# Expert pairs: wide weights by indirect gather, gathers without padding rows, gate and up products from f32r parts

## The chip, the cores and the metric

The kernel runs on one core of one Trainium2 chip. The metric is the device time of one execution in microseconds (us). Before the change three runs gave a median of 3015.25 us (3013.92 to 3015.65).

## The reference

Two transformer-like blocks work on 1024 tokens of width 1024, in float32. Each block is a mixer (a state-space scan and a Fourier mixer in the first, an S5 branch and a gated unit in the second) followed by a mixture of experts with 32 experts in 4 groups. The change is in the two mixtures only. Each token goes to the two best experts of its best group, so there are 2048 assignments per block, and every expert computes, for the rows it is given:

```python
p_top_grp, grp = lax.top_k(p_grp, 1)            # best of 4 groups
p_top, j_top = lax.top_k(p_exp, TOP_K_INNER)    # best 2 of its 8 experts
gate = p_top_grp * p_top / jnp.sum(p_top, axis=-1, keepdims=True)
hid = silu(xblk @ w_gate[e]) * (xblk @ w_up[e])     # 1024 -> 512
y = hid @ w_down[e]                                 # 512 -> 1024
out[token] += gate * y
```

Each expert has three weights of 2 MB (w_eg, w_eu, w_ed in the first block, w1, w3, w2 in the second).

## The kernel before

Everything runs in program order per engine with semaphores written out by hand; there is no planner. `moe_phase` (first block) and `mixed_moe` (second block) compute the routing: TensorE makes logits, VectorE a long chain of small steps that ends in the lists `idx_a` and `idx_b` (which rows to gather) and `ids` (which expert each unit of work takes), stored to `blk_dram`. Both then call `expert_pairs` (L1078 to L1346).

The assignments are cut into units. A wide unit has 128 rows, a narrow unit 64. A pair is one wide unit of one expert and one narrow unit of another, 192 row slots; slots with no assignment are padding and hold row 0. There are 18 pairs in the first block and 17 in the second; the count is read at run time (`pairs`).

The weights of a pair are nine pieces in nine buffers: `w_a[0..2]` (gate, up, down of the wide unit, 2 MB each) and `w_b[0..5]` (gate, up, down of the narrow unit, in halves of 1 MB). The pieces of the first pair are loaded during the routing. In the loop SP issues all nine, in one queue and a fixed order: wide gate, wide up, four narrow pieces, wide down, two narrow pieces. Each issue waits until the buffer has been used (`s_used`, or `s_wdl` for wide down).

TensorE does per pair: gate and up of the wide unit (`up_a`, float32 products of 128x512, each two passes, L1192), gate and up of the narrow unit (`up_b`, L1202), transposes of the hidden values and of the next wide rows (`rows_a`), the wide down product (`down_a`), the narrow down product (`down_b`), transposes of the next narrow rows (`rows_b`).

`down_a` already works from f32r parts: ScalarE copies the weight piece to f32r (`wd_h`, L1291), VectorE subtracts that from the piece (`wd_l`, L1326), and TensorE adds three f32r products: high by high, high by low, low by high (L1215, L1216, L1221).

VectorE also makes `hid_a` (L1323), which happens once per pair when gate and up are done, copies the transposed rows to SBUF (`rows_T`), and scales the results (`y_a` L1342, `y_b` L1345), which ScalarE stores to `yrows`. POOL gathers the rows of the next pair from `xr_dram` with two indirect DMAs (L1152).

Of the kernel before, what the change touches and what calls it, by code (L numbers as in the profile page):

```python
# [6 lines left out]
P = 128  # L7
D = 1024
SEQ = 1024
T = SEQ // P  # L10
# [9 lines left out]
POOL_DMA_SEMAPHORES = 6  # L20
# [18 lines left out]
def moe_phase(nc, tag, x_in, mod, norm_w, w_rg, b_rg, w_re, b_re, w_gate, w_up, w_down, yrows, pool_dma, keep):  # L39
# [11 lines left out]
    s_xb, s_ga = pool_dma[0:2], pool_dma[2:6]  # L51
    xr_half = xr_dram.rearrange("s (h d) -> (s h) d", h=2)
    with ExitStack() as ctx:
# [15 lines left out]
        idx_a, idx_b = (sb(n, [P, NB], I32) for n in ("idxa", "idxb"))  # L69
        x_a, x_b = sb("xa", [P, D]), sb("xb", [P, D // 2])  # L70
        w_a = [sb(f"wa{p}", [P, 2 * WF]) for p in range(3)]
        w_b = [sb(f"wb{p}", [P, WF]) for p in range(6)]
        s_wa = [sem(f"wa{p}") for p in range(3)]
        s_wb = [sem(f"wb{p}") for p in range(6)]
        ga_dram, ua_dram = (w.rearrange("e (p j) f -> e p (j f)", j=J) for w in (w_gate, w_up))
        gb_dram, ub_dram = (w.rearrange("e (h p j) f -> e h p (j f)", h=2, j=J // 2) for w in (w_gate, w_up))
        da_dram = w_down.rearrange("e (p c) d -> e p (c d)", c=JF)
        db_dram = w_down.rearrange("e (h p c) d -> e h p (c d)", h=2, c=2)

        def piece_a(e, p):  # L80
            return (ga_dram, ua_dram, da_dram)[p][e]
# [4 lines left out]
        with ExitStack() as c2:  # L86
# [59 lines left out]
            isbig, upper = sb2("isbig", [P, 1]), sb2("upper", [P, 1])  # L146
            idf = sb2("idf", [P, 4])
# [5 lines left out]
            ps_f = ps_q[:, 1, 0:2 * NB].rearrange("p (c i) -> p c i", c=2)  # L153

# [21 lines left out]
            s_ft, s_fi, s_step = sem("ft"), sem("fi"), sem("step")  # L176
# [3 lines left out]
            with nc.Block() as block:  # L180
                @block.sync
                def _(sp):
# [24 lines left out]
                def _(pool):  # L207
# [4 lines left out]
                    nc.gpsimd.iota(tokf[:, :], [[P, T]], base=0, channel_multiplier=1,  # L212
# [11 lines left out]
                    nc.gpsimd.tensor_copy(wr[:, :, NG:NG + NE].rearrange("p j (g e) -> p g j e", g=NG), wre[:, :, :, :]).then_inc(s_wrc, 1)  # L224
                    for r in range(RXS):
                        pool.wait_ge(s_sr[r], 16 * (T // RXS))
                    pool.wait_ge(s_fi, 2)
                    nc.gpsimd.indirect_dma_start(x_a[:, :], None, xr_dram,
                                                 bass.IndirectOffsetOnAxis(ap=idx_a[:, 0:1], axis=0)).then_inc(s_xb[0], 16)
                    nc.gpsimd.indirect_dma_start(x_b[:, :], None, xr_half,  # L230
                                                 bass.IndirectOffsetOnAxis(ap=idx_b[:, 0:1], axis=0)).then_inc(s_xb[1], 16)
# [35 lines left out]
                def _(pe):  # L267
# [48 lines left out]
                    last.then_inc(s_ft, 1)  # L316

                @block.vector
                def _(v):
# [141 lines left out]
                    link(nc.vector.tensor_scalar(upper[:, :], iota_p[:, :], SB - 0.5, None, ALU.is_gt))  # L461
# [14 lines left out]
                    nc.vector.tensor_copy(ids[:, :], idf[:, :]).then_inc(s_blk, 1)  # L476

        expert_pairs(nc, tag, w_a, w_b, s_wa, s_wb, piece_a, piece_b, NE, NF, xr_dram, xr_half, blk_dram, yrows, ident, s_xb, sem, idx_a, idx_b, x_a, x_b, mod[5 * D:6 * D])
# [3 lines left out]
def mixed_moe(nc, tag, mix, mod, norm_w, w_rg, b_rg, w_re, b_re, w_gate, w_up, w_down, final_w, x_out, yrows, pool_dma):  # L482
# [11 lines left out]
    s_xb, s_ga = pool_dma[0:2], pool_dma[2:6]  # L494
    xr_half = xr_dram.rearrange("s (h d) -> (s h) d", h=2)
    with ExitStack() as ctx:
# [12 lines left out]
        idx_a, idx_b = (sb(n, [P, NB], I32) for n in ("idxa", "idxb"))  # L509
        WF = J // 2 * NF  # L510
# [20 lines left out]
        with ExitStack() as c2:  # L531
# [52 lines left out]
            with nc.Block() as block:  # L584
                @block.sync
                def _(sp):
# [30 lines left out]
                def _(pool):  # L617
# [17 lines left out]
                    for r in range(RXS):  # L635
                        pool.wait_ge(s_sr[r], 16 * (T // RXS))
# [3185 lines left out]
```

## Time and profile before

| | |
|---|---|
| median of the runs | 3015.25 us |
| the profiled execution | 3012.52 us, span 3010.8 us |
| mean granted TensorE clock | 0.949 |
| TensorE busy | 2716.9 us, 90% of the span |
| VectorE busy | 1446.9 us, 48% |
| ScalarE busy | 768.4 us, 26% |
| POOL busy | 204.9 us, 7% |
| bytes moved by DMA | 799.95 MB, mean 266 GB/s |
| share of SP's queue | 694.08 MB, 60.8% of 16 engines |
| software queue (POOL) | 45.88 MB, 4.1% |

Busy times are sums of instructions; DMA shares are of the 16 DMA engines over the whole span. The expert loops stand out in the page's slices as two stretches (about 1020 to 1620 us and 2400 to 2960 us) with TensorE and DMA both near full.

### The profile page before, as it was taken

Reading aid. Unit: us, or ns where it says so; the run is one execution under the profiler, and the core shown is the slowest. Engines: PE = TensorE matmul, PEld = TensorE weight load, DVE = VectorE, ACT = ScalarE, POOL = GpSimd, SP = SyncE. Lnnn points to the kernel's source line nnn. Section 1 sums busy time; section 2 is a strip of 40 time slices with the busy share of each in tenths; the row PEclk is TensorE's granted clock in tenths of the full one; section 3 lists DMA queues with packets and bytes.
Section 4 is the critical chain, followed back from the end, with each engine's and each line's share of the span. In section 5 each row is a group of like instructions: output and inputs, shape, how many; then the busy total and the mean of one; then the engine's idle time right before and its main releaser. Section 6 shows DMA issues by size and latency. Waiting matters only on the chain. (4 is left out here: it accounts for less than half of the span.)

```text
span 3010.8 us, 36671 instructions
## 1 busy us (share of the span) xinstructions
PE 2716.9 (90%) x13982; PEld 1892.5 (63%) x13982; DVE 1446.9 (48%) x2054; ACT 768.4 (26%) x1116; POOL 204.9 (7%) x242
## 2 busy tenths in 40 slices
PE   4999996988798799999997899799779799999998
PEld 2788784765577555555553587688657655555554
DVE  3766365896633533332333755573445533323334
ACT  4223222653302012111212521234212121112112
POOL 0000000000000000000001121121000000000002
PEclk6999997999899899999998899899899899999999
DMA  6652374787734699999996414353652599999996
GB/s 244 243 179 77 104 270 144 221 266 283 271 116 178 273 424 425 424 424 426 425 424 251 127 50 108 77 125 108 234 193 99 220 395 424 424 425 426 424 424 252
DMA packets 276482, 799.95 MB, mean 266 GB/s; under 512 B 34164, under 2 KB 156592, under 8 KB 229784
## 3 DMA queue, kind: packets, MB, share of 16 engines
q1 hardware_dynamic: 234368, 694.08, 60.8%
q10 hardware_dynamic: 29112, 58.54, 5.3%
q0 software_dynamic: 12896, 45.88, 4.1%
q8 instruction: 71, 1.16, 0.2%
q14 instruction: 35, 0.29, 0.0%
HBM read 684.76 MB, written 113.67 MB: 265 GB/s over the span
## 5 line engine op out<-in xcount | busy, mean ns | idle before, releaser
L1192 PE MATMUL m_ps_ga<-m_wa,m_xTa 128*128 128x512 f32 x560 | 250.1, 600 | 0.8 <-issue 0.8
L1202 PE MATMUL m_ps_b<-m_wb,m_xTb 128*64 128x256 f32 x2240 | 249.5, 381 | 0.0
L1323 DVE TENSOR_TENSOR m_hida<-m_ps_ua,m_sila 128x512 f32<-128x512 f32 x35 | 24.2, 691 | 463.9 <-PE m_ps_ua L1192 463.9
L1192 PE MATMUL m_ps_ua<-m_wa,m_xTa 128*128 128x512 f32 x560 | 246.0, 592 | 0.0
L1763 PE MATMUL xp_acc<-xp_xh,xp_wh 128*128 128x512 f32 (+3 forms) x600 | 223.7, 373 | 6.9 <-DVE xp_xl L2046 6.9
L1288 ACT ACT_TABLE_LOAD x35 | 44.9, 1283 | 702.8 <-PE m_ps_ga L1192 702.8
L1202 PEld LDWEIGHTS m_ps_b<-m_wb,m_xTb 128*64 128x64 f32 x2240 | 157.8, 137 | 102.3 <-issue 26.5
L1764 PE MATMUL xp_acc<-xp_xl,xp_wh 128*128 128x512 f32 (+3 forms) x600 | 221.3, 369 | 0.0
L1765 PE MATMUL xp_acc<-xp_xh,xp_wl 128*128 128x512 f32 (+3 forms) x600 | 221.2, 369 | 0.0
L2942 PE MATMUL xq_acc<-xq_xh,xq_wh 128*128 128x512 f32 x448 | 181.2, 404 | 13.6 <-PEq L3011 6.4
L1192 PEld LDWEIGHTS m_ps_ua<-m_wa,m_xTa 128*128 128x128 f32 x560 | 106.4, 190 | 133.9 <-issue 133.9
L1326 DVE TENSOR_TENSOR m_wdl<-m_wa,m_wdh 128x2048 fp32r<-128x2048 f32 x70 | 157.1, 2286 | 62.6 <-ACT m_wdh L1291 62.6
L1192 PEld LDWEIGHTS m_ps_ga<-m_wa,m_xTa 128*128 128x128 f32 x560 | 105.5, 194 | 121.0 <-issue 121.0
L2943 PE MATMUL xq_acc<-xq_xl,xq_wh 128*128 128x512 f32 x448 | 178.8, 399 | 0.0
L2944 PE MATMUL xq_acc<-xq_xh,xq_wl 128*128 128x512 f32 x448 | 178.6, 399 | 0.0
L1291 ACT ACTIVATE m_wdh<-m_wa 128x2048 fp32r<-128x2048 f32 x70 | 130.0, 1904 | 169.8 <-DMA m_wa<-in_w_ed_dram 94.3
L1763 PEld LDWEIGHTS xp_acc<-xp_xh,xp_wh 128*128 128x128 f32 (+1 forms) x600 | 112.6, 188 | 29.4 <-issue 9.6
L1231 PE MATMUL m_ps_b<-m_wb,m_hTb 128*64 128x512 f32 x560 | 127.9, 598 | 0.0
L1215 PE MATMUL m_ps_y<-m_wdh,m_hTah 128*128 128x512 f32 x280 | 116.0, 414 | 10.7 <-DVE m_hTah L1329 10.6
L1765 PEld LDWEIGHTS xp_acc<-xp_xh,xp_wl 128*128 128x128 f32 (+1 forms) x600 | 112.5, 187 | 20.3
L1764 PEld LDWEIGHTS xp_acc<-xp_xl,xp_wh 128*128 128x128 f32 (+1 forms) x600 | 112.7, 188 | 19.8
L1216 PE MATMUL m_ps_y<-m_wdl,m_hTah 128*128 128x512 f32 x280 | 109.8, 392 | 0.0
(706 smaller groups left out, 4770.0 us busy)
## 6 DMA issues: line engine op xcount, KB each, us to landing
m_wa<-in_w_dram SPq DMA_DIRECT2D x51, 2048.0 KB, 17.5
m_wb<-in_w_dram SPq DMA_DIRECT2D x102, 1024.0 KB, 17.9
m_wa<-in_w_eg_dram SPq DMA_DIRECT2D x18, 2048.0 KB
m_wa<-in_w_eu_dram SPq DMA_DIRECT2D x18, 2048.0 KB, 16.3
m_wb<-in_w_eg_dram SPq DMA_DIRECT2D x36, 1024.0 KB, 17.4
m_wb<-in_w_eu_dram SPq DMA_DIRECT2D x36, 1024.0 KB, 22.2
m_wa<-in_w_ed_dram SPq DMA_DIRECT2D x18, 2048.0 KB, 26.8
m_wb<-in_w_ed_dram SPq DMA_DIRECT2D x36, 1024.0 KB, 20.7
```

The lines of the kernel that those rows point to most:

```text
L1192: last = nc.tensor.matmul(out[:, :], xT_a[:, j, :], w[:, k, :], start=(j == 0), stop=(j == J - 1))
L1202: last = nc.tensor.matmul(ps_b[c * SB:(c + 1) * SB, p // 2, :], xT_b[:, k, h * SB:(h + 1) * SB], w[:, k, c * HF:(c + 1) * HF], start=(h == ...
L1215: nc.tensor.matmul(o, hT_ah[:, k, :], w_h[:, c, cols], start=(k == 0), stop=False)
L1231: last = nc.tensor.matmul(ps_b[d * SB:(d + 1) * SB, :, :], hT_b[:, c, h * SB:(h + 1) * SB], w[:, c, d * NF:(d + 1) * NF], start=(k == 0), ...
L1291: nc.scalar.activation(wd_h[:, h, :], w_a[2][:, h * WF:(h + 1) * WF], ACT.Copy).then_inc(s_wdh, 1)
L1326: nc.vector.tensor_tensor(wd_l[:, h, :], w_a[2][:, h * WF:(h + 1) * WF], wd_h[:, h, :].bitcast(F32), ALU.subtract).then_inc(s_wdl, 1)
L1763: nc.tensor.matmul(o, h, xh[:, j, a:a + w], start=(j == 0), stop=False)
L1764: nc.tensor.matmul(o, h, xl[:, j, a:a + w], start=False, stop=False)
L1765: last = nc.tensor.matmul(o, l, xh[:, j, a:a + w], start=False, stop=(j == J - 1))
L2942: nc.tensor.matmul(o, wh[:, n % 2, j, :], x_h[:, j, tok], start=(j == 0), stop=False)
L2943: nc.tensor.matmul(o, wh[:, n % 2, j, :], x_l[:, j, tok], start=False, stop=False)
L2944: last = nc.tensor.matmul(o, wl[:, n % 2, j, :], x_h[:, j, tok], start=False, stop=(j == k - 1))
```

## The change

In `expert_pairs` and the two functions that call it:

- The wide pieces are no longer issued by SP. POOL gathers each with an indirect DMA: 128 rows of 16 KB, at row numbers `idx_w` (expert times 128 plus partition). Where a pair's wide expert is that of the pair before, or the pair is past the last, the number is made larger than the table, and an indirect DMA with `bounds_check` leaves such rows out. `idx_w` is made by a few more steps at the end of the routing (`spread`, `weight`, `again`). The first pair's wide pieces are gathered by POOL too.
- Padding slots of `idx_a` and `idx_b` now hold a number past the table (`PAD`), so that the gathers leave them out; `x_a` and `x_b` are set to zero once beforehand.
- Gate and up of the wide unit are computed from f32r parts, as down was. The two-slot buffer `wd_h`, `wd_l` becomes a ring (`ring_h`, `ring_l`) through which six halves go per pair: gate, up, down, two each. ScalarE makes the high part, VectorE the low part; a slot is filled again when TensorE has used it (`s_ring`). The first two halves of the next pair's gate are made at the end of a pair. The rows `xT_a` become `xT_ah` and `xT_al`.

The core of the diff:

```diff
@@ routing, both blocks
-                    nc.vector.tensor_copy(idx_a[:, :], ps_f[:, 0, :]).then_inc(s_fi, 1)
+                    nc.vector.tensor_scalar(idx_a[:, :], ps_f[:, 0, :], float(PAD), None, ALU.add).then_inc(s_fi, 1)
...
+                    nc.vector.tensor_scalar(spread[:, :], ident[:, 0:NB], idf[:, 0:1], None, ALU.mult).then_inc(s_spread, 1)
+                    v.wait_ge(s_we, 1)
+                    link(nc.vector.tensor_scalar(weight[:, :], ps_e, float(P), iota_p[:, 0:1], ALU.mult, ALU.add))
+                    link(nc.vector.tensor_tensor(again[:, 1:NB], weight[:, 1:NB], weight[:, 0:NB - 1], ALU.is_equal))
+                    link(nc.vector.scalar_tensor_tensor(out=again[:, 1:NB], in0=iota_s[:, 1:NB], scalar=npair[:, 0:1],
+                                                        in1=again[:, 1:NB], op0=ALU.is_ge, op1=ALU.add))
+                    link(nc.vector.scalar_tensor_tensor(out=idx_w[:, 1:NB], in0=again[:, 1:NB], scalar=8.0 * NE * P,
+                                                        in1=weight[:, 1:NB], op0=ALU.mult, op1=ALU.add))
...
@@ POOL during the routing
+                    for p in range(3):
+                        nc.gpsimd.indirect_dma_start(w_a[p][:, :], None, wide[p],
+                                                     bass.IndirectOffsetOnAxis(ap=first[:, 0:1], axis=0)).then_inc(s_wa[p], 16)
+                    nc.gpsimd.memset(x_a[:, :], 0.0).then_inc(s_zero, 1)
+                    nc.gpsimd.memset(x_b[:, :], 0.0).then_inc(s_zero, 1)
...
@@ expert_pairs, SP
-                    e_a = sp.value_load(blk_dram[0:1, bass.ds(4 * i, 1)], min_val=0, max_val=NE - 1)
-                    for p in range(2):
-                        sp.wait_ge(s_used, 12 * i + 2 * p + 2)
-                        sp.dma_start(w_a[p][:, :], piece_a(e_a, p)).then_inc(s_wa[p], 16)
...
-                    sp.wait_ge(s_wdl, 2 * i)
-                    sp.dma_start(w_a[2][:, :], piece_a(e_a, 2)).then_inc(s_wa[2], 16)
...
@@ expert_pairs, POOL
+                def weights(i, p):
+
+                    pool.wait_ge(s_wl, 6 * i + 2 * p + 8)
+                    pool.sem_inc(s_one, 1)
+                    nc.gpsimd.tensor_copy(row_w[p][:, :], idx_w[:, bass.ds(i + 1, 1)]).then_inc(s_rw[p], 1)
+                    pool.wait_ge(s_rw[p], i + 1)
+                    pool.sem_inc(s_one, 1)
+                    pool.indirect_dma_start(w_a[p][:, :], None, wide[p], bass.IndirectOffsetOnAxis(ap=row_w[p][:, :], axis=0),
+                                            bounds_check=NE * P - 1, oob_is_err=False).then_inc(s_wa[p], 16)
+
+                gather(1, 1, idx_a, row_a, xr_dram, x_a, s_xta, 0, SEQ)
+                with pool.Fori(0, n) as i:
+                    gather(i + 1, i + 1, idx_b, row_b, xr_half, x_b, s_xtb, 1, 2 * SEQ)
+                    for p in range(3):
+                        weights(i, p)
+                    gather(i + 2, i + 2, idx_a, row_a, xr_dram, x_a, s_xta, 0, SEQ)
...
@@ expert_pairs, TensorE
+                    for h in range(2):
+                        w_h, w_l = (w[:, h, :].rearrange("p (j f) -> p j f", f=NF) for w in (ring_h, ring_l))
+                        pe.wait_ge(s_wh, 6 * i + 2 * u + h + 1)
+                        for k in range(J // 2):
+                            j = h * J // 2 + k
+                            nc.tensor.matmul(out[:, :], xT_ah[:, j, :], w_h[:, k, :], start=(j == 0), stop=False)
+                            nc.tensor.matmul(out[:, :], xT_al[:, j, :], w_h[:, k, :], start=False, stop=False)
+                        pe.wait_ge(s_wl, 6 * i + 2 * u + h + 7)
+                        for k in range(J // 2):
+                            j = h * J // 2 + k
+                            last = nc.tensor.matmul(out[:, :], xT_ah[:, j, :], w_l[:, k, :], start=False, stop=(j == J - 1))
+                        last.then_inc(s_ring, 1)
...
@@ expert_pairs, ScalarE (in the loop)
+                    act.wait_ge(s_wa[1], 16 * i + 16)
+                    for h in range(2):
+                        act.wait_ge(s_ring, 6 * i + h + 1)
+                        high(1, h)
                     act.wait_ge(s_hida, i + 1)
                     nc.scalar.activation(sil_a[:, :], ps_ga[:, :], ACT.Silu).then_inc(s_sila, 1)
                     act.wait_ge(s_wa[2], 16 * i + 16)
                     for h in range(2):
+                        act.wait_ge(s_ring, 6 * i + h + 3)
+                        high(2, h)
...
                     nc.scalar.activation(sil_b[:, :], ps_b[:, 0, :], ACT.Silu).then_inc(s_silb, 1)
+                    act.wait_ge(s_wa[0], 16 * i + 32)
+                    act.wait_ge(s_ring, 6 * i + 5)
+                    high(0, 0)
+                    act.wait_ge(s_ring, 6 * i + 6)
+                    high(0, 1)
                     act.wait_ge(s_ya, i + 2)
...
@@ expert_pairs, VectorE (low: ring_l = w_a piece - ring_h)
+                    for h in range(2):
+                        low(1, h, 6 * i + h + 2)
+                    low(2, 0, 6 * i + 4)
...
                     nc.vector.tensor_tensor(hid_a[:, :], ps_ua[:, :], sil_a[:, :], ALU.mult).then_inc(s_hida, 1)
+                    low(2, 1, 6 * i + 5)
...
-                    rows_T(ps_x[:, :, :], xT_a, i + 1, s_xta, s_xTa)
+                    wide_T(i + 1)
...
                     nc.vector.tensor_tensor(y_a[:, :], ps_y[:, :], g2a[:, :], ALU.mult).then_inc(s_ya, 1)
+                    low(0, 0, 6 * i + 6)
...
+                    low(0, 1, 6 * i + 7)
```

## Rows read from the trace of the kernel before

**Rows 1.** DMA issues by line: tiles, queue, operation, count, KB, median us to landing.
```profile
m_wa<-in_w_dram SPq DMA_DIRECT2D x51, 2048.0 KB, 17.5
...
m_wa<-in_w_ed_dram SPq DMA_DIRECT2D x18, 2048.0 KB, 26.8
...
m_xa<-m_xr,m_rowa POOLq DMA_INDIRECT x35, 9.1
```

**Rows 2.** Windows in the first loop: stretch, busy us per engine, clock, DMA share, GB/s.
```profile
1200.00:1300.00 100.00, 100.00 (x485) 55.97 (x486) 33.59 (x34) 17.93 (x16) 6.95 (x12) 1.00 1.01 425
...
1500.00:1600.00 100.00, 97.86 (x466) 54.45 (x464) 32.62 (x33) 18.00 (x16) 6.95 (x12) 1.00 1.01 425
```

**Rows 3.** Timeline of VectorE, both loops: start, duration, instruction, idle before it.
```profile
1037.18 0.69 DVE L1323 TENSOR_TENSOR m_hida<-m_ps_ua,m_sila 128x512 f32<-128x512 f32 x1 [15.78 <-PE m_ps_ua L1192]
...
1069.76 0.69 DVE L1323 TENSOR_TENSOR m_hida<-m_ps_ua,m_sila 128x512 f32<-128x512 f32 x1 [13.11 <-PE m_ps_ua L1192]
...
1330.69 0.69 DVE L1323 TENSOR_TENSOR m_hida<-m_ps_ua,m_sila 128x512 f32<-128x512 f32 x1 [13.11 <-PE m_ps_ua L1192]
...
1346.03 1.22 DVE L1342 TENSOR_TENSOR m_yra<-m_ps_y,m_g2a 128x1024 f32<-128x1024 f32 x1 [2.42 <-PE m_ps_y L1221]
...
1364.01 0.69 DVE L1323 TENSOR_TENSOR m_hida<-m_ps_ua,m_sila 128x512 f32<-128x512 f32 x1 [13.11 <-PE m_ps_ua L1192]
...
2941.65 0.69 DVE L1323 TENSOR_TENSOR m_hida<-m_ps_ua,m_sila 128x512 f32<-128x512 f32 x1 [13.11 <-PE m_ps_ua L1192]
```

**Rows 4.** Waits, 1060 to 1600 us: who for whom, us in total, times, longest.
```profile
ACT m_wdh L1291 <- DMA m_wa<-in_w_ed_dram: 94.3, 17, 7.1
```

**Rows 5.** End of the first loop: timeline, and one window.
```profile
1597.13 7.13 PE L1202 MATMUL m_ps_b<-m_wb,m_xTb 128*64 128x256 f32 x64
1597.33 0.69 DVE L1323 TENSOR_TENSOR m_hida<-m_ps_ua,m_sila 128x512 f32<-128x512 f32 x1 [13.11 <-PE m_ps_ua L1192]
...
1616.01 0.75 PE L1183 MATMUL m_ps_x<-m_ident,m_xb 128*128 128x128 f32 x4
...
1605.00:1610.00 5.00, 4.34 (x24) 3.61 (x23) 3.73 (x6) 0.00 (x0) 0.00 (x0) 1.00 0.00 0
```

**Rows 6.** Timeline of TensorE, gate and up of one pair.
```profile
1088.32 7.03 PE L1192 MATMUL m_ps_ga<-m_wa,m_xTa 128*128 128x512 f32 x16
...
1102.15 2.16 PE L1202 MATMUL m_ps_b<-m_wb,m_xTb 128*64 128x256 f32 x18
```

**Rows 7.** Timeline of TensorE, first and last of ten product starts in `down_a`.
```profile
1306.91 0.40 PE L1216 MATMUL m_ps_y<-m_wdl,m_hTah 128*128 128x512 f32 x1
...
1308.96 0.63 PE L1221 MATMUL m_ps_y<-m_wdh,m_hTal 128*128 128x512 f32 x2
```

**Rows 8.** Groups by line, 1130 to 1650 us: busy us, mean ns, idle before.
```profile
L1326 DVE TENSOR_TENSOR m_wdl<-m_wa,m_wdh 128x2048 fp32r<-128x2048 f32 x30 | 67.4, 2287 | 36.0 <-ACT m_wdh L1291 36.0
L1291 ACT ACTIVATE m_wdh<-m_wa 128x2048 fp32r<-128x2048 f32 x30 | 55.7, 1905 | 91.1 <-DMA m_wa<-in_w_ed_dram 91.1
L1288 ACT ACT_TABLE_LOAD x14 | 18.0, 1283 | 262.8 <-PE m_ps_ga L1192 262.8
L1152 POOL DMA_INDIRECT m_xb<-m_xr,m_rowb x14 | 13.8, 983 | 11.0 <-POOL m_rowb L1149 11.0
L1152 POOL DMA_INDIRECT m_xa<-m_xr,m_rowa x14 | 13.6, 969 | 11.2 <-POOL m_rowa L1149 11.2
```

**Rows 9.** Timeline ahead of the loops, first block, then second.
```profile
1009.14 1.15 POOL L228 DMA_INDIRECT m_xa<-m_xr,m_idxa  x1 [56.15 <-DVE m_idxb L465]
...
1010.32 0.33 ACTq L263 DMA_DIRECT2D m_blk<-m_ids  x1
...
1016.23 1.95 PE L1237 MATMUL m_ps_x<-m_ident,m_xa 128*128 128x128 f32 x8 [8.45 <-PEq L180]
...
1021.10 3.78 PE L1192 MATMUL m_ps_ga<-m_wa,m_xTa 128*128 128x512 f32 x4 [0.42 <-issue]
...
2400.36 8.94 PE L1192 MATMUL m_ps_ga<-m_wa,m_xTa 128*128 128x512 f32 x16 [0.38 <-issue]
```

More of the change, by code:

```diff
@@ L146, in moe_phase @@
             isbig, upper = sb2("isbig", [P, 1]), sb2("upper", [P, 1])
+            spread, weight, again = (sb2(n, [P, NB]) for n in ("spread", "weight", "again"))
             idf = sb2("idf", [P, 4])
@@ L316, in _ @@
                     last.then_inc(s_ft, 1)
+                    pe.wait_ge(s_spread, 1)
+                    nc.tensor.matmul(ps_e, ones[:, :], spread[:, :], start=True, stop=True).then_inc(s_we, 1)
                 @block.vector
@@ L509, in mixed_moe @@
         idx_a, idx_b = (sb(n, [P, NB], I32) for n in ("idxa", "idxb"))
+        idx_w, first = sb("idxw", [P, NB], I32), sb("first", [P, 1], I32)
         WF = J // 2 * NF
@@ L547, in mixed_moe @@
                 sb2(n, [P, NE]) for n in ("nbig", "nsml", "thr", "bend", "send", "bst", "sst", "sbase", "bbase", "early"))
-            half, npair, over, gain, later, isbig, upper = (sb2(n, [P, 1]) for n in ("half", "npair", "over", "gain", "later", "isbig", "upper"))
+            half, npair, over, gain, later, isbig, upper = (
+                sb2(n, [P, 1]) for n in ("half", "npair", "over", "gain", "later", "isbig", "upper"))
+            spread, weight, again = (sb2(n, [P, NB]) for n in ("spread", "weight", "again"))
             idf, ids = sb2("idf", [P, 4]), sb2("ids", [P, 4], I32)
@@ L731, in _ @@
                     last.then_inc(s_ft, 1)
+                    pe.wait_ge(s_spread, 1)
+                    nc.tensor.matmul(ps_e, ones[:, :], spread[:, :], start=True, stop=True).then_inc(s_we, 1)
                 @block.vector
@@ L1106, in expert_pairs @@
         s_used = sem("used")
-        s_row = [sem(f"row{r}") for r in range(2)]
+        s_row, s_rw = [sem(f"row{r}") for r in range(2)], [sem(f"roww{p}") for p in range(3)]
+        s_sta, s_stb = sem("sta"), sem("stb")
         s_xta, s_xtb, s_xTa, s_xTb = (sem(k) for k in ("xta", "xtb", "xTa", "xTb"))
@@ L1162, in _ @@
-                for r in range(2):
-                    pool.wait_ge(s_xb[r], 16 * n + 16)
+                    pool.indirect_dma_start(x[:, :], None, src, bass.IndirectOffsetOnAxis(ap=row[:, :], axis=0),
+                                            bounds_check=rows - 1, oob_is_err=False).then_inc(s_xb[r], 16)
+                def weights(i, p):
[6 more added lines that the diff above has]
+                                            bounds_check=NE * P - 1, oob_is_err=False).then_inc(s_wa[p], 16)
```

189 lines of the change are left out of this document (106 added, 83 removed).

## The prediction

> **What bounds the kernel now.** I read, in this order, the windows, the timeline of VectorE, the timeline of TensorE inside a pair, the landing times of the DMAs, and the end of a loop. The change touches the two expert loops (18 pairs in the first block, 17 in the second, counted by the issues: 18 of the first block's down weights, 51 for the second's three wide pieces [rows 1]). In the windows the reader is to see two engines full at once: TensorE 98 to 100 of 100 us at a granted clock of 1.00, and DMA share 1.01 at 425 GB/s [rows 2]. Which one ends last is told by the distance between two `m_hida` instructions, one per pair: 32.6 us at first (1069.76 less 1037.18), 33.3 us from the tenth pair on (1364.01 less 1330.69) [rows 3]. 33.3 us is the DMA pace: a pair moves nine weight pieces, 12.58 MB, gathers 192 rows (0.79 MB) and stores as many, 14.16 MB, and at 425 GB/s that is 33.3 us. 32.6 us is TensorE's own pace, while the weights loaded ahead last. Where TensorE then waits is seen in ScalarE's wait for the down piece (94.3 us in 17 pairs) and in that piece's landing of 26.8 us [rows 1, 4]: its parts must be split before `down_a`. At the end of the loop DMA is already empty from 1605 on, while products run to 1616.8 [rows 5]: the one queue finishes early because its late piece is not the last one.
>
> **The change part by part, one pair.**
>
> *Gate and up from parts.* Now the two take from 1088.32 to 1102.15, 13.83 us (32 passes, 0.43 us each) [rows 6]. Afterwards they are 48 f32r products; the same kind in `down_a` follows each 0.228 us (1306.91 to 1308.96, nine steps) [rows 7]: 10.94 us. That takes 2.9 us from TensorE's 32.6. The price is four more ACT copies of 1.91 us and four more DVE subtractions of 2.29 us per pair, and one more subtraction for `xT` (1.22 us, as `m_yra` of the same size) [rows 3, 8]. ACT goes from about 6 to 14 us per pair and DVE from 11 to 21, sums from these rows, so neither is full; but the ring holds two halves, so a half can be split only when the one before the last is used up. That chain is copy 1.91, subtraction 2.29 and some 0.4 of semaphores, 4.6 us; a half lasts 12 x 0.228 = 2.74 us, and the low parts are wanted after another 8 x 0.228 = 1.82, that is after 4.56. The two meet to 0.1 us. I charge 0.2 us per pair, bounds 0 and 1.4 (a table load of 1.28, now ahead of silu [rows 8], falling into the chain). TensorE's pace: 32.6 - 2.9 + 0.2 = 29.9, taken as 30.0.
>
> *Bytes.* Counting the reference's routing on the inputs that it draws gives 2048 real rows in each block, against 18 x 192 and 17 x 192 gathered, and two pairs of the first block (the 10th and the 12th) whose wide expert is that of the pair before, none in the second. A pair then moves 12.58 + 0.79 stored + 0.47 to 0.49 gathered = 13.84 MB: 32.6 us, still more than 30.0. So DMA stays the bound, 0.7 us quicker per pair, except around a repeated expert, which leaves out 6.29 MB (14.8 us).
>
> *Where the pieces come free.* A wide piece is now free when its second low half is made, not when the products have read it: the gate buffer right at the start of a pair instead of 7 us later, the up buffer at 10, down at 17. Each has its own wait in POOL's queue, so the wide pieces no longer stand in line with the narrow ones in SP's. A wide gather is not in the trace. On POOL the nearest are the row gathers, 0.97 us with rows of 4 KB, 0.98 with 2 KB [rows 8], so the time goes by rows, not bytes: I take 1.0 us plus copy and wait of 1.1, bounds 1.0 and 3.9 (a row split in four); five gathers keep POOL under half of the pair. In its queue `gather` of the next wide rows stands behind the wait for the down piece, at 17 us, but those rows are wanted a pair later. On ScalarE the copies of the next gate piece stand ahead of the y stores, and behind their wait for that piece wait only these stores, which VectorE asks for a pair later; SP only loses issues. Landing: between 4.9 us (2 MB at full rate) and 26.8 (the down piece in SP's line). I take 10.5, from the x_a gather: 128 packets of 4 KB on the software queue land in 9.1 us although SP's queue is full [rows 1]; that is 8 packets per engine, each taking turns with one of 8 or 16 KB (0.3 to 0.6 us at a sixteenth of 425 GB/s), plus some 3 us fixed. Eight packets of 16 KB: 8 x (0.6 + 0.3) + 3. The Trainium skill, "DMA: Bandwidth & Descriptors", section on queues, rings and completion order, says that each DMA engine goes round the queues that have work, a packet each. The trace agrees, 9.1 against 26.8 us at the same load; strict order by issue would give the last rival's time.
>
> *Slack.* The gate piece must land about 20 us after it is freed (its copies follow `down_a`), up and down 20 to 22; 12.6 with the issue fits. So the narrow pieces, in SP's queue with what DMA is left, are late first: the fourth one, last of `up_b`. DMA works without a gap from about 14 us after the first gate product (until then it has moved one wide piece and two gathers, 2.9 MB). By then the second pair's fourth narrow piece needs about 9 MB, 21 us, so it lands at 35 to 36; it is wanted at 2.1 (cold first pair: 1021.10 to 1037.18 less 0.2, against 13.83 [rows 3, 6, 9]) + 30.0 + 10.9 + 5.4 = 48.4. Slack 12 us, shrinking by 2.6 per pair.
>
> *Before the loops.* The extra `xT` subtraction stands ahead of the first gate product: 2400.36 moves by 1.2 us, twice [rows 9]. The five small DVE steps and one product for `idx_w` (1.8 us by their like) run while the block list is stored and the engines meet, 1010.3 to 1016.2 [rows 9]: nothing, 3.6 us in both blocks if uncovered. POOL's iota, memsets and three first gathers lie in the 56 us that POOL waits for the indices [rows 9]: nothing, and below nothing is excluded, since the indices end that wait. The 12.58 MB loaded ahead are the same.
>
> **Sum, from the profiled execution's 3012.5 us (span 3010.8).** First block: now 1021.10 to 1616.76, 595.7 us. After: 1.2 + 2.1 + 18 x 30.0 = 543.3, plus waits for DMA: slack 12 is gone by the seventh pair, 6 us by the ninth; filled to 12 again at the tenth and twelfth, 3.5 us by the eighteenth. 552.8: 42.9 less. Second block: now 2400.36 to 2961.1 (the last `m_hida` at 2941.65 plus the 19.4 it has to the end in the first block, 1597.33 to 1616.76 [rows 3, 5]), 560.7. After: DMA throughout. 16 x 12.58 MB of weights, 12.6 of stores, 8.0 of gathers are 222 MB; less 2.9 moved early and 2.1 (two last pieces) 217 MB, 510.9 us; plus 14, plus 14.3 from the fourth narrow piece to the end (19.6 less three quarters of 7.13 [rows 5]), plus 1.2: 540.4, 20.3 less. Together 63: 2949.3, and 2952 on the scale of the runs, whose median is 2.7 above the profiled execution.
>
> **Rivals.**
>
> *The split sets the pace*: the table load or a late copy costs 1.4 us per pair, 31.4. First block 3.3 + 18 x 31.4 = 568.5, no DMA wait; second 3.3 + 17 x 31.4 + 6.5 of DMA waits = 543.6. Less 44: 2971. For it: 0.1 us of room. Against: today's copies need no load of their own [rows 8]. The Trainium skill, "GPSIMD Engine Reference", key points, says that POOL shares its SBUF interfaces with VectorE and contends with instructions of two SBUF inputs. The new subtractions are such; by that rule two of them per pair, each held up for most of a gather's 0.97 us, would give this rival's time. No row shows a gather beside one.
>
> *Skipped rows still cost their transfer* (the change does not do what it says): pace 33.3 again; first block 543.3 + 41, second 513.3 + 38. Less 21, from the earlier buffers alone: 2994. No row shows an index out of range.
>
> *Slower: a wide buffer's round is longer than the pair.* Each wide piece has one buffer: freed, issued 2.1, landed L, copied in two halves, subtracted: L + 8.7. With L = 26.8 as the down piece today [rows 1] 35.5 us for each pair that is not a repeat: 36 + 15 x 35.5 + 2 x 30 and 34 + 16 x 35.5 against 1156.4, 74 slower: 3089. It decides from L = 24.4 on. Against it the 9.1 us of the row gathers; for it that 2 MB have never gone through this queue.
>
> **Numbers.** Forecast 0.53, split 0.16, no skip 0.11, slower 0.12, the rest (mixtures, a few per cent less DMA rate) 0.08. The forecast's own range is 2932 (slack 20 instead of 12) to 2968. The range 2930 to 3000 takes in the first two rivals. Within 0.2% (6 us, what a measurement can tell) 0.03; faster 0.84; slower 0.13.
>
> **What would show it.** `m_hida` distances of 30 us, then 32.6, 30 again after the 10th pair; in the second block 32.6 from the seventh on; DMA at 425 GB/s; gate and up in 11 us; wide gathers landing in 10 to 14 us; software-queue bytes up by some 195 MB. Distances of 33 throughout, landings over 24 us, or waits of gate products for `ringl` would prove it wrong.

## The result, and the profile after

The changed kernel takes 2985.4 us (median of four runs, 2983.0 to 2986.9); the kernel before took 3014.6 in the same session. The ratio is 0.990, 95% interval 0.9888 to 0.9912: 29 us faster, where 63 were forecast. The profiled execution took 2986.4 us (span 2984.6).

Two parts came out as predicted. The first is the bytes. The page's queues of the kernel after (queue: packets, MB, share of 16 engines):

```profile
q1 hardware_dynamic: 219248, 473.87, 43.8%
q0 software_dynamic: 29168, 241.21, 19.7%
```

The software queue carries 195 MB more, as forecast. The second is that the wide pieces land soon enough. The landings (tiles, queue, operation, count, KB where given, median us), which answer to [rows 1]:

```profile
m_wb<-in_w_dram SPq DMA_DIRECT2D x102, 1024.0 KB, 24.5
m_wb<-in_w_ed_dram SPq DMA_DIRECT2D x36, 1024.0 KB, 23.3
m_wa<-in_w_dram,m_roww POOLq DMA_INDIRECT x51, 14.3
m_xa<-m_xr,m_rowa POOLq DMA_INDIRECT x37, 16.3
```

A wide gather lands in 14.3 us (10.5 taken, 24.4 would have made the kernel slower), a narrow piece of half the size only in 24. By the rule of the Trainium skill that the prediction drew on ("DMA: Bandwidth & Descriptors", queues and rings: a packet from each queue in turn) a queue of 16 KB packets would get twice what a queue of 8 KB packets gets, if what the rule calls a packet is what the profile counts as one. 2 MB in 14.3 against 1 MB in 24.5 us goes that way, but it is no test: a narrow piece also stands behind those issued before it in SP's queue.

The loops look otherwise than forecast. Windows of the kernel after, as [rows 2] (stretch, busy us of PE, PEld, DVE, ACT, POOL, granted clock, DMA share, GB/s):

```profile
1100.00:1200.00 100.00, 96.76 (x538) 66.25 (x534) 63.78 (x49) 45.20 (x31) 28.41 (x31) 0.97 1.01 425
1300.00:1400.00 100.00, 100.00 (x562) 70.00 (x558) 67.68 (x54) 47.12 (x32) 31.92 (x33) 1.00 0.90 351
1500.00:1600.00 100.00, 92.50 (x516) 64.48 (x514) 66.88 (x52) 46.09 (x34) 29.21 (x32) 0.98 0.82 336
2500.00:2600.00 100.00, 93.80 (x504) 63.31 (x503) 63.19 (x48) 43.58 (x30) 25.33 (x30) 0.95 1.01 421
```

DMA share 1.01 and TensorE with gaps: a loop that waits for DMA. Only about the two repeats of block 1 (1300 to 1400) is it the other way round. (The third row reaches past the end of the loop at 1592.5, so its lower DMA share is not the loop's.) VectorE's `m_hida`, one per pair, as [rows 3], and then the issue of the last two narrow pieces, and TensorE between the second and third of these `m_hida`:

```profile
1096.62 0.68 DVE L1412 TENSOR_TENSOR m_hida<-m_ps_ua,m_sila 128x512 f32<-128x512 f32 x1
1127.02 0.68 DVE L1412 TENSOR_TENSOR m_hida<-m_ps_ua,m_sila 128x512 f32<-128x512 f32 x1
...
1163.46 0.68 DVE L1412 TENSOR_TENSOR m_hida<-m_ps_ua,m_sila 128x512 f32<-128x512 f32 x1
```
```profile
1111.13 2.05 SPq L1175 DMA_DIRECT2D m_wb<-in_w_ed_dram  x2
```
```profile
1139.53 1.94 PE L1287 MATMUL m_ps_b<-m_wb,m_hTb 128*64 128x512 f32 x8
1144.71 3.68 PE L1287 MATMUL m_ps_b<-m_wb,m_hTb 128*64 128x512 f32 x8 [3.24 <-DMA m_wb<-in_w_ed_dram]
1148.32 1.13 PE L1234 MATMUL m_ps_x<-m_ident,m_xb 128*128 128x128 f32 x4
```

A pair takes 30.4 us (1127.02 less 1096.62) or, where it waits, 36.4 (1163.46 less 1127.02). What is late is the last narrow down half, issued at 1111 to 1113 and landed at 1144.7. After the 3.24 us wait the same eight products take 3.68 us in place of 1.94: the granted clock is 1.00 before the wait (1139.5 to 1141.5) and 0.50, the lower of its two levels (1.2 and 2.4 GHz), from 1144.7 to 1149.5. Distances of block 1 from the first pair on: 30.1, 30.4, 30.4, **36.4**, 30.2, **35.6**, 30.2, **37.3**, six of 30.1 to 30.4, **36.5**, 30.1, 30.4. In block 2 they go between 30.1 and 37.1 throughout, mean 32.64. The rows of the waits (who for whom, us, times, longest, 1060 to 1600 us), where [rows 4] had ScalarE's 94.3 us (the first is POOL waiting for the subtraction that frees a wide buffer):

```profile
POOL m_roww L1197 <- DVE m_ringl L1396: 113.8, 34, 4.6
...
PEld m_ps_b L1287 <- DMA m_wb<-in_w_ed_dram: 17.6, 5, 4.3
...
PE m_ps_b L1287 <- DMA m_wb<-in_w_ed_dram: 13.4, 4, 3.4
```

The end of the second loop, as [rows 5]: VectorE's last `m_hida` and TensorE's last products of the loop, then the window of DMA (in its second row a share of 0.23 and 89 GB/s: the tail of what had been 424):

```profile
2918.76 0.68 DVE L1412 TENSOR_TENSOR m_hida<-m_ps_ua,m_sila 128x512 f32<-128x512 f32 x1
```
```profile
2934.95 0.75 PE L1234 MATMUL m_ps_x<-m_ident,m_xb 128*128 128x128 f32 x4
```
```profile
2905.00:2915.00 10.00, 9.91 (x43) 7.71 (x43) 7.64 (x5) 7.29 (x6) 6.43 (x4) 1.00 1.03 424
2915.00:2935.00 20.00, 20.00 (x127) 12.87 (x125) 13.12 (x12) 7.65 (x5) 3.61 (x6) 1.00 0.23 89
```

From first gate product to last product, block 1 went from 595.7 to 571.8 us (1020.75 to 1592.5), block 2 from 560.7 to 555.6 (2380.13 to 2935.7); what lies between the blocks grew by 4.0. Forecast were 552.8 and 540.4, each with 1.2 for what stands ahead of the loop.

### The profile page after: what moved, and what is told of

The parts are those of the page before. It is cut to its first block and busy times, and to the rows that moved or that the text cites. A ratio compares the mean times of both kernels' runs of the same rounds, so it can differ in the third digit from the quotient of the medians.

```text
span 2984.6 us, 39013 instructions
## 1 busy us (share of the span) xinstructions
PE 2659.2 (89%) x14546; PEld 2003.0 (67%) x14546; DVE 1818.7 (61%) x2245; ACT 1089.5 (37%) x1295; POOL 461.6 (15%) x468
## 5 line engine op out<-in xcount | busy, mean ns | idle before, releaser
L1396 DVE TENSOR_TENSOR m_ringl<-m_wa,m_ringh 128x2048 fp32r<-128x2048 f32 x214 | 489.3, 2287 | 142.8 <-ACT m_ringh L1340 141.8
L1340 ACT ACTIVATE m_ringh<-m_wa 128x2048 fp32r<-128x2048 f32 x214 | 409.6, 1915 | 287.2 <-PE m_ps_y L1277 184.1
L1287 PE MATMUL m_ps_b<-m_wb,m_hTb 128*64 128x512 f32 x560 | 142.2, 646 | 31.1 <-DMA m_wb<-in_w_dram 17.7
L3020 POOL TENSOR_TENSOR xq_wl<-xq_raw,xq_wh 128x1024 fp32r<-128x1024 f32 (+1 forms) x32 | 78.2, 2444 | 361.0 <-ACT xq_wh L3015 361.0
L1244 PE MATMUL m_ps_ga<-m_ringh,m_xTah 128*128 128x512 f32 x280 | 118.3, 422 | 2.4 <-issue 2.4
L1187 POOL COPY m_rowb<-m_idxb 128x1 int32 x35 | 69.4, 1983 | 322.5 <-PE m_ps_x L1234 322.5
L1271 PE MATMUL m_ps_y<-m_ringh,m_hTah 128*128 128x512 f32 x280 | 116.4, 416 | 0.0
L2024 DVE TENSOR_TENSOR xp_wl<-xp_raw,xp_wh 128x1024 fp32r<-128x1024 f32 (+1 forms) x29 | 34.7, 1197 | 132.0 <-ACT xp_wh L1933 132.0
L1245 PE MATMUL m_ps_ga<-m_ringh,m_xTal 128*128 128x512 f32 x280 | 113.9, 407 | 0.0
L1287 PEld LDWEIGHTS m_ps_b<-m_wb,m_hTb 128*64 128x64 f32 x560 | 37.6, 143 | 110.8 <-issue 68.4
## 6 DMA issues: line engine op xcount, KB each, us to landing
m_wb<-in_w_dram SPq DMA_DIRECT2D x102, 1024.0 KB, 24.5
m_wb<-in_w_ed_dram SPq DMA_DIRECT2D x36, 1024.0 KB, 23.3
```

The costliest lines, as they stand in the source:

```text
L1244: nc.tensor.matmul(out[:, :], xT_ah[:, j, :], w_h[:, k, :], start=(j == 0), stop=False)
L1271: nc.tensor.matmul(o, hT_ah[:, k, :], w_h[:, c, cols], start=(k == 0), stop=False)
L1287: last = nc.tensor.matmul(ps_b[d * SB:(d + 1) * SB, :, :], hT_b[:, c, h * SB:(h + 1) * SB], w[:, c, d * NF:(d + 1) * NF], start=(k == 0), ...
L1340: nc.scalar.activation(ring_h[:, h, :], w_a[p][:, h * WF:(h + 1) * WF], ACT.Copy).then_inc(s_wh, 1)
L1396: nc.vector.tensor_tensor(ring_l[:, h, :], w_a[p][:, h * WF:(h + 1) * WF], ring_h[:, h, :].bitcast(F32), ALU.subtract).then_inc(s_wl, 1)
```

## The experiments

Three theories stood at first. **1, order**: the wide pieces come early, the narrow down halves late, so the reserve lies in the wrong pieces. **2, bytes**: the DMA engines are full, and only the byte count matters. **3, split and clock**: the chain of copies and subtractions and TensorE's lower clock make the long pairs. "Loop 1" and "loop 2" below are the time from a block's first `m_hida` to its last, from the profiled execution; the kernel before had 560.2 and 525.4, the one after 539.6 and 522.2. Ratios are to the kernel before on the same chip. The edits are shown in short form: each line stands for its counterpart in the kernel, and helper lines are left out.

**One queue in order of need** (wide pieces from SP again; then the same with a branch past a repeated expert's loads):

```diff
+ for p in range(2): sp.wait_ge(s_wl, 6 * i + 2 * p + 2); sp.dma_start(w_a[p], piece_a(e_a, p))
  for p in range(4): sp.wait_ge(s_used, 6 * i + p + 1);  sp.dma_start(w_b[p], piece_b(e_b, p))
+ sp.wait_ge(s_wl, 6 * i + 6); sp.dma_start(w_a[2], piece_a(e_a, 2))
  for p in (4, 5): ...
```

> The changed kernel with the wide pieces issued by SP again, in one queue with the narrow ones and in the order in which they are needed (gate, up, four narrow, down, two narrow); a repeated expert is loaded again. Theory 1 (two queues put the reserve in the wrong pieces: the wide ones come early, the narrow down halves late): the first pairs of block 1 go at 30.4 us, no 36 us pair before the eighth, and TensorE hardly waits for the narrow down halves (17.6 us after, under 5 here); block 2 ends some 9 us earlier, because the last piece to land is needed later; block 1 pays up to 15 us for the two repeats (6.29 MB at 420 GB/s). Sum 2980 to 2992. Theory 2 (bytes at the rate of the DMA engines are the bound, the order does nothing): 2985.4 + 15 = 3000. Theory 3 (the chain of the split and the lower clock set the pace, not the DMAs): 2985, with pairs of 36 us left where they are.

> The one queue in order of need, and SP branches past the three wide loads of a repeated expert (it adds 16 to the semaphore in their place). Theory 1 (order of the pieces): block 1 loses the stalls ahead of the repeats, about 13 us, block 2 about 9 us of its tail and up to 4 us more if the one queue moves 425 GB/s in place of 421: 2958 to 2965. Theory 2 (bytes and rate alone, which are those of the changed kernel): 2985, within 4 us. Theory 3 (split chain and clock): 2985, within 4 us.

Measured: 2995.3 (ratio 0.9945, 0.9933 to 0.9957), loops 555.0 and 524.1; with the branch 2990.0 (0.9922, 0.9909 to 0.9935), loops 545.3 and 526.4. Theory 1 fails: the narrow down halves are no longer late, and nothing is won; with the same bytes the kernel with the branch is some 6 us slower than the changed one. The wait moved to the wide pieces (first row, the kernel with one queue, 2450 to 2850 us), and the long pairs became even ones of 33.3 us, at a clock of 1.00 and the same full DMA (second row, window of the one with the branch). These two kernels change more than the order, though: in SP's one queue a piece whose buffer is free stands behind one whose buffer is not, and in the first pairs of the one with the branch DMA moves only 365 and 370 GB/s (1035 to 1060 and 1060 to 1080 us), against 402 and 428 in the changed kernel.

```profile
ACT m_ringh L1351 <- DMA m_wa<-in_w_dram: 60.3, 11, 5.9
```
```profile
2500.00:2600.00 100.00, 91.41 (x511) 63.12 (x510) 62.86 (x49) 44.44 (x30) 13.44 (x13) 1.00 1.01 424
```

That also takes the clock out: 0.95 in the same stretch of the changed kernel, 1.00 here, and loop 2 no shorter. The lower clock follows the waits (0.50 after the 3.24 us wait above); where it stays at 1.00, no time is won.

**Nothing wide to load** (every index out of bounds), and **the two queues held in order** (POOL waits for the fifth narrow piece's landing ahead of the gate gather):

```diff
- again = (weight[1:] == weight[:-1])
+ again = (weight[1:] == weight[1:])
```
```diff
+ if p == 0: pool.wait_ge(s_wb[4], 16 * i + 16)
```

> The changed kernel with every wide index of the loops out of bounds, so that no wide weights are loaded after the first pair (all pairs are computed with the first expert's wide weights). It shows TensorE's own pace with the split, beside DMA engines that have half as much to move. Theories 1 and 2 (DMA sets what is above 30.4 us a pair): all pairs at 30.2 to 30.6 us, granted clock 1.0 in both loops, 2985 - 24 (excess over 30.4 in block 1) - 36 (block 2) = 2925. Theory 3 (split chain and clock): pairs of 34 to 37 us remain, over 2960.

> The changed kernel with one more wait on POOL: the gate gather of the next pair is issued only when the fifth narrow piece of this pair has landed, so the two queues keep nearly the order of need and the skip stays. Theory 1: the narrow down halves land earlier (median landing under 20 us in place of 22, none over 30), the 36 us pairs ahead of the repeats go, block 2 gains less than with one queue: 2965 to 2975. Theories 2 and 3: 2985, within 4 us, or slower, since the wide pieces start later.

Without wide loads: all distances 30.1 to 30.7 us in both loops, means 30.37 and 30.46, clock 1.00. Time 2961.9, but its changed rows give block 2 an 18th pair; less 30.5 that is 2931, against 2925 expected. Theory 3 falls: the split alone keeps 30.4. Row of its window:

```profile
1350.00:1450.00 100.00, 100.00 (x552) 68.47 (x552) 69.45 (x54) 48.68 (x32) 30.61 (x31) 1.00 0.67 250
```

The held queues: 3018.6 (1.0015, 1.0004 to 1.0027), loops 558.1 and 535.1: some 35 us slower than the changed kernel, 44 to 54 beyond what theory 1 gave. DMA moves 401 to 415 GB/s in the stretches of block 2, where the changed kernel has 417 to 426; that fits a queue that is left with less to do by each wait for a landing.

**The parts alone.** Split without the byte savings (one queue, no skip, `PAD = 0`), and byte savings without the split (gate and up as before, wide pieces and rows by the changed gathers):

> Gate and up from f32r parts, and nothing else of the change: wide pieces by SP in one queue, no repeated expert left out, padding rows gathered again, so the bytes are those of the kernel before. Theory A (the DMA engines, busy without a gap, set the time; order and queue change nothing): TensorE's pace falls from 32.6 to 30.4 us a pair and nothing comes of it, every pair takes 33.3 us (14.15 MB at 425 GB/s): 3008 to 3016. Theory B (the parts are worth something each, and add up): it shows a good part of the 29 us, 3000 or less.

> The gathers, the skip and the left-out padding rows of the change, with gate and up in plain fp32 as before. Theory A: TensorE's pace of 32.6 us a pair is now the bound, so only what before had over 32.6 goes (the pairs of 33.3: 6 us in block 1, 4 in block 2): 3002 to 3008, all pairs within 0.1 of 32.6, DMA share under 1. Theory B: with the f32r part alone it adds up to the 29 us of both.

Measured: split alone 3017.5 (1.0004, 0.9996 to 1.0013): nothing. Bytes alone 3008.7 (0.9974, 0.9965 to 0.9984): 8 us. Together they give 30 (the ratio 0.990): the parts don't add up. With the split alone nearly every pair takes 33.4 us at full DMA, TensorE with gaps (first row); with the bytes alone every pair of block 1 takes 32.6, TensorE full and, past the repeats, DMA with room (second row). In block 2 that forecast missed: four pairs take 33.0 to 35.6, and loop 2 is 528.5, 3 us longer than before the change. There the two queues move 417 to 425 GB/s at a full DMA share (third row), and a pair's 13.84 MB take 32.6 to 33.2 us at that rate:

```profile
1250.00:1350.00 100.00, 91.28 (x511) 63.03 (x511) 62.77 (x49) 44.31 (x31) 13.44 (x12) 1.00 1.01 424
```
```profile
1250.00:1350.00 100.00, 100.00 (x469) 55.49 (x468) 33.14 (x34) 17.58 (x15) 24.20 (x32) 1.00 0.93 371
```
```profile
2720.00:2820.00 100.00, 98.34 (x464) 54.41 (x463) 32.62 (x33) 17.59 (x15) 23.06 (x30) 1.00 1.00 417
```

**Byte savings undone one at a time, and bytes added.**

```diff
- again = (weight[1:] == weight[:-1])
+ again = 0 * weight[1:]
```
```diff
- PAD = 4 * SEQ
+ PAD = 0
```
```diff
  act.dma_start(y_v[i][0:P], y_a).then_inc(s_sta, 16)
+ act.dma_start(spare_v[i][0:P], y_a).then_inc(s_sta, 16)
```

> The changed kernel, but a repeated expert's wide weights are loaded again (12.6 MB more in block 1). Theory A: the DMA engines never idle in block 1 (1.01 share in all of it, 0.93 and 0.95 after), its mean pair goes from 31.7 to 32.6, +15: 2995 to 3003; block 2 is as it was. Theory B' (the skip comes too late in the block to be worth anything): 2985.

> The changed kernel with the padding rows gathered again (1408 rows of 4 KB in block 1, 1216 in block 2: 5.8 and 5.0 MB). Theory A (while the DMA engines are behind, every byte costs its time at 424 GB/s; where they are ahead, none does): 11.7 us in block 2, 7 to 10 in block 1: 3003 to 3009. Rival (a left-out row costs its transfer all the same, or the pace is not set by bytes): 2985.

> The changed kernel with the wide result rows of each pair stored a second time, to a spare tensor, from the same queue (0.52 MB a pair, 8.9 MB in block 2; a byte count raised with no instruction of TensorE, VectorE or POOL touched). Theory A: 1.24 us a pair where the DMA engines are behind, so 21 us in block 2 and 11 to 15 in block 1: 3017 to 3022. Rival (the late pieces come from order, POOL or the clock, not from the byte count): 2985 to 2990.

Without the skip: 3007.9 (0.9974, 0.9963 to 0.9985), 22 us more than the change by the ratios; loop 1 557.0, DMA full in all of it. With padding rows: 3005.6 (0.9962, 0.9948 to 0.9976), 19 more; loops 548.8 and 528.5. Rows stored twice: 3024.2 (1.0033, 1.0022 to 1.0044), 40 more, loops 554.6 and 539.8. So 12.6, 10.8 and 18 MB cost 22, 19 and 40 us, where no work of TensorE or VectorE in the loop was touched. At 424 GB/s these bytes alone take 30, 25 and 43 us. One time lies within what theory A gave, two lie 2 and 5 us over it.

**The same 6.29 MB in the middle and at the end.** The last pair of either block has no wide rows; its index can be taken before the limit to 31, so that its load is out of bounds. And in block 2 the ninth pair's load is left out:

```diff
+ spread = ident[:, 0:NB] * idf[:, 0:1]
  idf[:, 0:2] = min(idf[:, 0:2], NE - 1)
- spread = ident[:, 0:NB] * idf[:, 0:1]
```
```diff
+ again[:, 8:9] = 1.0
```

> The changed kernel, and the wide weights of the last pair, which has no wide rows in either block, are left out too (its index is taken before it is limited to 31, so it is out of bounds): 6.29 MB less at the end of each block. If only the sum of bytes counted: 30 us less, 2956. Theory A with buffers (bytes count only where a later pair still waits for them): the last pieces are loaded when the last 37 us pair is over, so 1 to 3 us a block at most: 2980 to 2985.

> The changed kernel, but in block 2 the wide weights of the ninth pair aren't loaded (it is computed with those of the eighth): the same 6.29 MB as at the end of block 2, left out in the middle. Theory A with buffers: the pairs after it go at 30.4 us for some seven pairs, 13 to 15 us less in block 2: 2970 to 2973. If the loss were order or clock and not bytes: one 37 us pair less at most, 2979 or more.

At the end: 2985.0 (0.9894, 0.9876 to 0.9912), loops 535.4 and 524.2: nothing, though DMA is only 0.68 busy there (first row; the changed kernel has 1.03 and 424 GB/s in that stretch). In the middle: loop 2 510.2, 12.0 less, six distances in a row of 30.1 to 30.5; the five runs spread from 2971.6 to 2985.8, median 2979.7 (0.9884, 0.9869 to 0.9899), so that the time itself shows only some 5 us, not set apart from the change by its interval, and doesn't exclude the rival's 2979. What speaks for theory A here is loop 2 of one profiled execution, the fastest of the five. Second row: its window, TensorE full, clock 1.00.

```profile
2905.00:2915.00 10.00, 9.91 (x44) 7.79 (x45) 7.61 (x5) 6.95 (x6) 6.42 (x4) 1.00 0.68 245
```
```profile
2620.00:2720.00 100.00, 99.70 (x568) 69.73 (x565) 68.17 (x55) 46.41 (x32) 32.53 (x34) 1.00 0.97 401
```

So a byte was worth its time where DMA was behind and a later pair still waited for it, and nothing at the end.

**The empty pair moved to the middle**, which leaves nothing of the reference out, beside the changed kernel once more. Ahead of the loops every position from the fifth (block 2: ninth) pair on moves by one pair, the last pair's to there, and the tables of experts likewise (`M` is 4 and 8):

```diff
+ posf += PAIR * (posf > PAIR * M - 0.5) - PAIR * (npair - M) * (posf > PAIR * (npair - 1) - 0.5)
+ turn = iota_p - (iota_p > M - 0.5) + (npair - M) * (iota_p == M)
- early = bend <= iota_p
+ early = bend <= turn
```

> The changed kernel with its last pair, which has no wide rows in either block and whose wide weights are left out, taken fifth in block 1 and ninth in block 2 (the other pairs follow in their order; positions and tables are computed for the new order ahead of the loops). Theory A with buffers: in block 1 the three 36 us pairs ahead of the repeats go (6.0 + 5.2 + 6.9 = 18 us over 30.4), in block 2 as much as when the ninth was left out (12 us); the new VectorE instructions ahead of the loops cost 1 to 3 us a block: 2955 to 2963. If the late pieces of block 1 come from another cause than the byte count: only block 2 gains, 2972 to 2976.

> The changed kernel itself beside the one with the empty pair in the middle, on the same chip: a ratio to before of 0.989 to 0.991 as it was, so that the two can be set side by side; its 36 to 37 us pairs at other places by one or two pairs, the mean of block 2 at 32.6 again.

Measured: 2977.6 (0.9885, 0.9868 to 0.9902) against 2988.3 (0.9910, 0.9892 to 0.9927) for the changed kernel on that chip: the fastest by its median of the kernels that compute the whole reference, with intervals that overlap, and 15 us over the 2963 expected. Loops 529.6 and 512.4 against 536.1 and 523.6. Block 2 gained 11 us of the 12 expected; block 1 only 6.5 to 10 of the 18. Up to its ninth pair the distances hold 7.7 us over 30.37 each, where the changed kernel had 13.0 and 17.7 in its two profiles, so that late pairs of block 1 go when bytes go there too. Of the 37.3 us pair that is left ahead of the repeats the cause wasn't shown. DMA moves 406 and 410 GB/s between 1050 and 1250 us with TensorE full; that fits a load left out too early, when pieces wait for their buffers.

**Result rows of padding not stored** (indirect stores from POOL, padding out of bounds):

```diff
- act.dma_start(y_v[i][0:P], y_a)
+ pool.indirect_dma_start(yrows, IndirectOffsetOnAxis(row_y), y_a, None, bounds_check=..., oob_is_err=False)
```

> The changed kernel with fewer bytes in another place: the result rows of padding are no longer stored (each pair's rows go out by an indirect store from POOL whose padding rows are out of bounds; 1408 rows of 3456 in block 1 and 1216 of 3264 in block 2, 5.8 and 5.0 MB). Theory A: 5.0 MB at 424 GB/s is 11.7 us off block 2, and in block 1 the first nine pairs gain some 7: 2965 to 2972. If not the bytes but the pace of TensorE, the order or the clock bound the loops, nothing comes of it, or it is slower by the work on POOL: 2985 or more.

Measured: 3008.5 (0.9978, 0.9968 to 0.9988), a miss of 40 us. Half of it lies ahead of the loops: the first gate product comes at 1032.0 in place of 1020.8, and the second block's another 14 us later. New index steps and two more first transfers stand ahead of both; they weren't priced apart. The loops, 540.5 and 523.3, are as they were with 5 MB less each. In one queue the stores stand ahead of the next wide pieces, which now land after 23.8 us, and DMA moves only 412 GB/s (rows from 2450 to 2850 us); what lowered the rate wasn't separated, so this run says little for or against theory A.

```profile
DMA packets 20996, 164.79 MB, mean 412 GB/s; under 512 B 3952, under 2 KB 3952, under 8 KB 7134
...
m_wa<-in_w_dram,m_roww POOLq DMA_INDIRECT x38, 23.8
```

## Why the prediction was half right

**Right**: DMA as the bound after the change, its pace of 32.6 us a pair (block 2: 32.64), 30 us about the repeats, the bytes, the wide landings short enough, the setting free of the wide buffers. That the time lies in the stated range, 2930 to 3000, is luck: the range took in two rivals that the runs refute, and the forecast's own range, 2932 to 2968, missed it by 17 us.

**Wrong, the step that failed: "Slack 12 us, shrinking by 2.6 per pair".** It was worked out from when the second pair's fourth narrow piece lands (35 to 36 us after the first gate product) and is wanted (48.4). It landed after 39.3. The issue of this piece for the second, third and fourth pair with its time to landing, and `up_b` of the same pairs, which wants the piece after three quarters:

```profile
L1172 SPq DMA_DIRECT2D m_wb<-in_w_eu_dram x1: 337/337/337, 1040.9 to 1040.9; - x1
DMA to landing us min/median/max: 19.1/19.1/19.1
...
L1172 SPq DMA_DIRECT2D m_wb<-in_w_eu_dram x1: 333/333/333, 1071.3 to 1071.3; - x1
DMA to landing us min/median/max: 22.1/22.1/22.1
...
L1172 SPq DMA_DIRECT2D m_wb<-in_w_eu_dram x1: 333/333/333, 1101.7 to 1101.7; - x1
DMA to landing us min/median/max: 28.2/28.2/28.2
```
```profile
1064.15 7.13 PE L1259 MATMUL m_ps_b<-m_wb,m_xTb 128*64 128x256 f32 x64
...
1094.54 7.13 PE L1259 MATMUL m_ps_b<-m_wb,m_xTb 128*64 128x256 f32 x64
...
1124.90 7.13 PE L1259 MATMUL m_ps_b<-m_wb,m_xTb 128*64 128x256 f32 x64
```

Its slack was 9.5, 6.5 and 0.4 us, where 12 less 2.6 a pair gives 12, 9.4 and 6.8; that of the last down half, read in the same way, was 13.4, 5.9 and -3.2. So the reserve shrank some two to three times as fast as forecast. One thing that the forecast left out can be seen: at 1140.3 the fifth pair's wide up piece has landed, while the fourth pair's last down half, already late, lands at 1144.7.

By the distances the loop waits from the fourth pair on, and has lost 13.0 to 17.7 us by the ninth where 6 were forecast; at 2.6 a pair that is a reserve of 0 to 5 us. The kernel before had said so in rows that I had: its distances go from 32.6 to 33.3 at the tenth pair [rows 3], and nine pairs at 0.7 are 6 us, not 12. I took the reserve from one piece's schedule and didn't hold it against that. The piece named as late first, the last of `up_b`, wasn't it either; it was the last down half. But the runs with one queue, where another piece is late, took 260.8 and 262.9 us from the first `m_hida` to the ninth (the changed kernel 260.7 and 256.0): a better order of these pieces alone, as far as it was tried, wins nothing. More buffers for the narrow pieces weren't tried. The kernel before took 260.8 too. Up to the ninth pair the change gained 0 to 5 us, and most of what block 1 won came from the repeats on. In block 1 waits came to 23.3 us (539.6 less 17 x 30.37) against 9.5 forecast: 14 of the 34 us missed in the two blocks.

**The tail**: "14.3 from the fourth narrow piece to the end" put the last bytes to use at once, about 9 us ahead of the end. In fact the last pieces land early: the rate runs down from 2915 on (318, 151 and 46 GB/s in steps of 2.5 us, 3 us at full rate), so that full work ends at some 2918, 17.7 us ahead of the last product, where the forecast left 9.3 (14.3 less 5 for the two pieces behind). Leaving out 6.29 MB more there did nothing. These are 8 us.

**The rate**: 425 GB/s was taken over from one queue; with two, block 2 goes at 417 to 426, 421 in its middle. On 217 MB that is 5 us. With the tail it makes 13 of the 15 us that block 2 missed.

**TensorE's pace**: 30.4, not 30.0. Gate and up of a pair take 11.7 us in place of 10.9 (1082.85 to 1094.54). The products follow each 0.234 us in place of the 0.228 taken (1083.16 to 1084.80, seven steps), which is 0.3 us a pair, and the weight loads of up wait for the ring's low halves, 5.8 us in 17 pairs: the forecast's own sign of being wrong, small and on up instead of gate. ScalarE now loads its tables twice a pair in place of once; what that adds to these waits wasn't tried. 0.4 x 17 distances of block 1 are 6 us. The rival that the split sets the pace (31.4) falls by the kernel without wide loads.

**The rivals on rows and buffers** fall too. A left-out row costs next to nothing: in the second block of the kernel without wide loads (2450 to 2850 us) the engines made some 5950 packets beyond the 16 of each DMA, all under 512 B, and the software queue's share of 5.0% over what its 6.84 MB would take at the price that 9.44 MB had in the kernel before (5.9%) is 0.7% of 16 engines, some 8 ns a packet (an estimate from these figures), where a 4 KB row takes some 160. And putting the padding rows back costs 19 us. That a wide buffer's round is longer than the pair needed landings of 24.4 us; they took 14.3.

So the expected gain went off into DMA time: TensorE's 2.2 us a pair are real, but over the 17 pairs of block 2 and the first nine of block 1 the DMA engines, not TensorE, set the mean pace. The split is worth 22 us only because the bytes fell, and the byte savings 30 (25 with one queue: 1.0004 less 0.9922) only because TensorE got faster.

## What to carry to other kernels

Where two engines are both full, shortening one shows nothing until the other gives way too: price the parts together, by the pace of each engine in turn, and not as a sum. Read the reserve from the trace before, as the number of rounds until the pace changes times the difference of the two paces, and hold every schedule worked out against it (here 6 us by that, 12, 0 to 5 found). Bytes that were spared paid only where a later round still waited for them: spread what can be skipped over a loop, away from its start and its end.

## What the runs showed of the hardware

POOL slows down beside VectorE. Groups by line of the changed kernel, 1130 to 1650 us (busy us, mean ns, idle before):

```profile
L1396 DVE TENSOR_TENSOR m_ringl<-m_wa,m_ringh 128x2048 fp32r<-128x2048 f32 x86 | 196.7, 2287 | 55.6 <-ACT m_ringh L1340 55.6
...
L1200 POOL DMA_INDIRECT m_wa<-in_w_eg_dram,m_roww x14 | 35.5, 2538 | 12.3 <-POOL m_roww L1197 12.3
...
L1187 POOL COPY m_rowb<-m_idxb 128x1 int32 x14 | 28.7, 2048 | 137.2 <-PE m_ps_x L1234 137.2
...
L1340 ACT ACT_TABLE_LOAD x14 | 18.0, 1283 | 79.7 <-issue 79.7
L1353 ACT ACT_TABLE_LOAD x14 | 18.0, 1283 | 0.3
...
L1200 POOL DMA_INDIRECT m_wa<-in_w_ed_dram,m_roww x15 | 15.2, 1016 | 13.1 <-POOL m_roww L1197 13.1
...
L1197 POOL COPY m_roww<-m_idxw 128x1 int32 x43 | 7.9, 185 | 99.8 <-DVE m_ringl L1396 99.7
```

The same copy of 128 numbers takes 0.19 us on one line and 2.05 on another, the issue of a gather 1.02 or 2.54, by whether a subtraction of VectorE runs beside it. In one pair the slow copy starts at 1083.35 behind a subtraction of 1083.16 to 1085.44, and takes 2.14 us; the gate gather's issue starts at 1088.45 behind one of 1088.25 to 1090.54, and takes 2.98. Two pairs later the same line's issue starts at 1154.42, 0.3 us ahead of a subtraction, and takes 1.01. The rule that the prediction cited from the Trainium skill ("GPSIMD Engine Reference", key points: POOL and VectorE share SBUF interfaces, and instructions of VectorE with two SBUF inputs contend) is seen here, the subtractions having `m_wa` and `m_ringh` as inputs, but on POOL's side: the subtractions keep 2287 ns, as before [rows 8], and without wide loads the pace stays at 30.4 us.

A gather whose rows are 16 KB issues in the 1.0 us of one with 4 KB rows [rows 8], and two DMA queues together move about 1% less than one (421 against 424 GB/s).
